# Narrow matmuls in twos on the two row halves, and the running sums of the decays moved into that stage

## The reference

```python
def _rwkv_bidir(u, v_first, vres, w0, w2, a0, a2, g2, k_k, k_a, r_k, gn_g, gn_b):
    r, k, v, wd_f, wd_b, ad_f, ad_b, gd = _split(u, [RW, RW, RW, 64, 64, 64, 64, 128])
    if vres is None: v_first = v
    else:
        v0, v1, v2 = vres
        v = v + (v_first - v) * jax.nn.sigmoid(v0 + (v @ v1) @ v2)   # v1: 512 x 32, v2: 32 x 512
    g = jax.nn.sigmoid(gd) @ g2
    kk = heads(k * k_k)
    kk = kk * lax.rsqrt(jnp.sum(kk * kk, -1, keepdims=True) + 1e-12)
    def direction(d, wd, ad, reverse):
        wl = w0[d] + jnp.tanh(wd) @ w2[d]                            # w2[d]: 64 x 512
        decay = jnp.exp(-jnp.exp(-jax.nn.softplus(-wl) - 0.5))
        a = jax.nn.sigmoid(a0[d] + ad @ a2[d])                       # a2[d]: 64 x 512
        kd = heads(k * (1.0 + (a - 1.0) * k_a))
        y = _wkv_scan(rh, heads(decay), kd, vh, kk, heads(a), reverse)
```

## Time and profile before

| | us |
|---|---|
| median of 3 runs (lowest, highest) | 4052.82 (4042.91, 4060.68) |
| the profiled execution | 4066.26 |
| its span in the profile | 4064.1 |
| TensorE busy | 3447.5 (85%) |
| VectorE busy | 1516.6 (37%) |
| ScalarE busy | 775.2 (19%) |
| mean granted TensorE clock | 0.91 |

### The profile page before, as it was taken

One profiled execution on the slowest core, in us unless ns is written; L12 is line 12 of the kernel. 1 busy time (PEld: TensorE's weight loads), 2 busy tenths in 40 slices (PEclk: granted clock), 3 DMA queues, 4 the chain that ended last, 5 costly groups with the idle time before them and its releaser, 6 DMA issues. The chain is left out here.

```text
span 4064.1 us, 74254 instructions
## 1 busy us (share of the span) xinstructions
PE 3447.5 (85%) x32128; PEld 2321.4 (57%) x32128; DVE 1516.6 (37%) x2765; ACT 775.2 (19%) x1578; POOL 329.0 (8%) x499
## 2 busy tenths in 40 slices
PE   4899899958856998898868847679989899999998
PEld 0666798754435666898645424447657744444443
DVE  2343555441122444454421132355456621144411
ACT  3112222121101113222111111013342210010000
POOL 0000221001110001220011110000023100000000
PEclk7999799968977997999969978889999999999999
DMA  8200300139972001101079932010010032222221
GB/s 297 77 32 23 126 5 5 43 119 376 397 279 86 32 16 76 76 4 41 5 290 373 409 110 73 16 44 21 21 54 1 1 122 74 73 72 73 70 59 47
DMA packets 178106, 418.33 MB, mean 103 GB/s; under 512 B 32661, under 2 KB 125205, under 8 KB 149253
## 3 DMA queue, kind: packets, MB, share of 16 engines
q1 hardware_dynamic: 158821, 379.68, 25.3%
q0 software_dynamic: 8736, 17.32, 1.6%
q10 hardware_dynamic: 10240, 16.79, 1.3%
HBM read 397.01 MB, written 50.54 MB: 110 GB/s over the span
## 5 line engine op out<-in xcount | busy, mean ns | idle before, releaser
L3213 PE MATMUL ps<-h_lat,wt 128*128 128x512 f32 x704 | 304.4, 595 | 5.9 <-ACT h_lat L3270 5.9
L1971 PE MATMUL ps<-e_w,e_xt 128*64 128x256 f32 x1792 | 236.3, 423 | 75.7 <-DMA e_w<-in_moe_w 75.6
L1971 PEld LDWEIGHTS ps<-e_w,e_xt 128*64 128x64 f32 x1792 | 156.4, 153 | 179.0 <-issue 98.8
L708 PE MATMUL ps<-h,win 128*128 128x264 f32 x960 | 232.7, 396 | 17.3 <-DVE pad L857 15.7
L3213 PEld LDWEIGHTS ps<-h_lat,wt 128*128 128x128 f32 x704 | 134.5, 191 | 175.8 <-issue 174.4
L708 PEld LDWEIGHTS ps<-h,win 128*128 128x128 f32 x960 | 180.5, 193 | 67.7 <-issue 39.1
L2078 DVE TENSOR_TENSOR e_hid<-ps,e_silu 64x256 f32<-64x256 f32 x64 | 39.3, 614 | 416.3 <-ACT e_silu L2037 416.3
L3170 PE MATMUL ps<-h_lat,wt 128*128 128x512 f32 x384 | 169.0, 598 | 10.9 <-DMA wt<-in_w_in 10.9
L3231 PE MATMUL ps<-ff_up,wt 128*128 128x512 f32 x352 | 152.2, 592 | 0.0
L1284 PE MATMUL ps<-inv,nt 48*48 48x48 f32 x3520 | 129.9, 207 | 12.6 <-issue 11.0
L1388 DVE COPY_PREDICATED inv<-level,ps 112x384 f32<-112x384 int32 x176 | 103.5, 588 | 85.8 <-PE ps L1284 77.6
(11 more groups left out here) (566 smaller groups left out, 6441.9 us busy)
## 6 DMA issues: line engine op xcount, KB each, us to landing
e_w<-in_moe_w SPq DMA_DIRECT2D x168, 1024.0 KB, 13.5
wmod<-in_w_mod SPq DMA_DIRECT2D x24, 1024.0 KB, 14.2
early<-in_moe_w SPq DMA_DIRECT2D x24, 1024.0 KB, 16.5
wt<-in_w_up SPq DMA_DIRECT2D x22, 1024.0 KB, 5.1
y_rows<-e_y ACTq DMA_DIRECT2D x128, 128.0 KB
win<-in_w_in SPq DMA_DIRECT2D x10, 1536.0 KB, 6.6
wt<-in_w_in SPq DMA_DIRECT2D x12, 1024.0 KB, 7.7
wt<-in_w_down SPq DMA_DIRECT2D x16, 704.0 KB, 4.8
```

The lines of the kernel that those rows point to most:

```text
L708: last = pe.matmul(ps[:, 7, 0:HT], lhsT=ring[(s + 1) % 2][:, i, o:o + P], rhs=k.h[:, i, h * HT:(h + 1) * HT], start=(i == 0), stop=(i == K ...
L1971: last = pe.matmul(ps[half, 2 + z, 0:EH], lhsT=xt[z][:, f, :], rhs=w[:, f, :], start=(f == 0), stop=(f == KD - 1))
L3213: last = pe.matmul(o, lhsT=w[:, i, m % 2 * P:(m % 2 + 1) * P], rhs=hl[:, i, :], start=(i == 0), stop=(i == KD - 1))
```

## The change

In `rwkv_prep`:

- The slots come in another order: `low` first, alone, then fourteen pairs: `sig` (4), `mix` (2), `rate` (4), `kk` (2), `att` (2). The two slots of a pair have their operands on different row halves. For `sig` and `rate` these are the two directions of one tile of channels. For `mix`, `kk` and `att` the operands are made twice, on rows from 0 and from 64: `v2` is loaded twice, `v1` is loaded twice into a tile of 96 columns (the 32 in the middle blank), `sel` has its 12 columns twice among 128, so `v_low` and `prep_root` come out on both halves.
- The matmuls of a pair alternate: first half of the positions of both slots, then the second half. Before a pair starts, both of its slots must be free.
- The sums stand between `sig` and `mix`. The squares of the attention output follow the `sig` evictions. The square root stands on ScalarE after the `mix` evictions, the tanh of `decay_in` first of all.
- The eight scans are done here, each after its `sig` eviction; VectorE's subtraction for `v` stands after the fourth. The reciprocal stands after the update of the first tile of `v`.

In `wkv` the scans and ScalarE's two waits on them are gone.

```diff
-        slots = ([("rate", d, m) for d in range(2) for m in range(RT)] + [("low", 0, 0)]
-                 + [("mix", 0, m) for m in range(RT)] + [("sig", d, m) for d in range(2) for m in range(RT)]
-                 + [("kk", 0, i) for i in range(RT)] + [("att", 0, h) for h in range(H_A)])
+        slots = ([("low", 0, 0)] + [("sig", d, m) for m in range(RT) for d in range(2)]
+                 + [("mix", m % 2, m) for m in range(RT)] + [("rate", d, m) for m in range(RT) for d in range(2)]
+                 + [("kk", i % 2, i) for i in range(RT)] + [("att", h % 2, h) for h in range(H_A)])
...
-                sp.dma_start(v1[:, :, :], a["rwkv_v1"][0].rearrange("(t p) n -> p t n", p=P)).then_inc(small_in, 16)
-                sp.dma_start(v2[:, :], a["rwkv_v2"][0]).then_inc(small_in, 16)
+                for b in (0, E):
+                    sp.dma_start(v2[b:b + LOW, :], a["rwkv_v2"][0]).then_inc(low_in, 16)
+                sp.wait_ge(low_blank, 1)
+                for b in (0, E):
+                    sp.dma_start(v1[:, :, b:b + LOW], a["rwkv_v1"][0].rearrange("(t p) n -> p t n", p=P)
+                                 ).then_inc(low_in, 16)
...
+                def pair(t):
+                    for x in (t, t + 1):
+                        if x >= 3:
+                            pe.wait_ge(act_emptied if by_act[x - 3] else dve_emptied, upto(x - 3))
+                    for h in range(2):
+                        hs = slice(h * HT, (h + 1) * HT)
+                        for x in (t, t + 1):
+                            l, r = operands(*slots[x])
+                            last = pe.matmul(two(x)[:, h, :], lhsT=l, rhs=r[:, hs], start=True, stop=True)
+                            if h:
+                                last.then_inc(slot_made, 1)
+                pe.wait_ge(low_in, 16 * 4)
...
+                for t in range(1, len(slots), 2):
+                    if t == MIX:
+                        sums()
+                        pe.wait_ge(act_emptied, 1)
...
+                    pair(t)
...
+                def scan(t):
+                    kind, d, m = slots[t]
+                    dve.wait_ge(act_emptied, t + 1)
+                    o, keep = sig[d][:, m, :], k.reset[:, d:d + T]
+                    if d:
+                        o, keep = o[:, ::-1], keep[:, ::-1]
+                    dve.tensor_tensor_scan(o, keep, o, 0.0, ALU.mult, ALU.add).then_inc(scanned, 1)
...
-                        if c < 2:
-                            act.wait_ge(scanned, RT * (d + 1))
...
-                    for f in range(RT):
-                        o, m = sig[d][:, f, :], k.reset[:, d:d + T]
-                        if d:
-                            o, m = o[:, ::-1], m[:, ::-1]
-                        dve.tensor_tensor_scan(o, m, o, 0.0, ALU.mult, ALU.add).then_inc(scanned, 1)
```

More of the change, by code:

```diff
@@ L947, in two @@
             return ps[:, 2 * (t % 3):2 * (t % 3) + 2, 0:HT]
[L948 to L951, removed]
+        with k.stage("low_in", "v_out", "v_in", "tanh_made", "gate_made", "att_squared", "keyed", "summed", "rooted",
+                     "inverted", "slot_made", "act_emptied", "dve_emptied", "y_blank", "low_blank", "sel_set", "eps_set",
+                     "spread_set", "scanned", "pool_chain", "prep_chain") as (
+                block, low_in, v_out, v_in, tanh_made, gate_made, att_squared, keyed, summed, rooted, inverted,
+                slot_made, act_emptied, dve_emptied, y_blank, low_blank, sel_set, eps_set, spread_set, scanned,
+                pool_steps, steps):
             @block.sync
@@ new lines, in sums @@
+                def sums():
+                    pe.wait_ge(att_squared, H_A)
+                    pe.wait_ge(keyed, RT)
+                    pe.wait_ge(sel_set, H_A + RT)
+                    for h in range(2):
+                        for n in range(H_A + RT):
+                            last = pe.matmul(ps[:, 6 + h, 0:HT], lhsT=sel[:, n, :, :].rearrange("p b e -> p (b e)"),
+                                             rhs=sq[:, n, h * HT:(h + 1) * HT], start=(n == 0), stop=(n == H_A + RT - 1))
+                    last.then_inc(summed, 1)
@@ new lines, in operands @@
+                def operands(kind, d, m):
+                    c, b = slice(m * P, (m + 1) * P), slice(64 * d, 64 * d + 64)
+                    if kind == "rate":
+                        return k.a2[b, c], rate_in[b, :]
+                    if kind == "sig":
+                        return k.w2[b, c], decay_in[b, :]
+                    if kind == "mix":
+                        b = slice(E * d, E * d + LOW)
+                        return v2[b, c], low[b, :]
+                    b = slice(E * d, E * d + H_A + H_B)
+                    if kind == "kk":
+                        return spread[b, 2 * m:2 * m + 2, :].rearrange("p b n -> p (b n)"), root[b, :]
+                    return few[b, m:m + 1].to_broadcast([H_A + H_B, P]), root[b, :]
@@ new lines, in _ @@
+                pe.wait_ge(low_in, 16 * 4)
+                for h in range(2):
+                    for i in range(RT):
+                        last = pe.matmul(two(0)[0:E + LOW, h, :], lhsT=v1[:, i, :], rhs=v[:, i, h * HT:(h + 1) * HT],
+                                         start=(i == 0), stop=(i == RT - 1))
+                last.then_inc(slot_made, 1)
+                pe.wait_ge(tanh_made, 1)
+                for t in range(1, len(slots), 2):
+                    if t == MIX:
+                        sums()
+                        pe.wait_ge(act_emptied, 1)
+                    if slots[t][0:2] == ("kk", 0) and slots[t][2] == 0:
+                        pe.wait_ge(inverted, 1)
+                        pe.wait_ge(spread_set, 1)
+                    pair(t)
```

120 lines of the change are left out of this document (44 added, 76 removed).

## The result

| | before | after |
|---|---|---|
| median (range) of 20 runs each, us | 4052.07 (4041.16 to 4063.03) | 4067.72 (4052.05 to 4076.09) |
| ratio after / before, 95% interval | | 1.0034 [1.0024, 1.0045] |
| profiled execution, us (span) | 4066.26 (4064.1) | 4076.09 (4074.0) |
| stage in front of the scan, layer 0 / 1, us | 56.2 / 56.0 | 63.0 / 62.7 |
| from its end to the first matmul on `bet`, us | 15.8 / 15.8 | 13.2 / 13.2 |

The medians lie 15.6 us apart; the ratio says 0.34%, 14 us. That is inside the 0.5% that the prediction took for no change, but the interval of the ratio excludes 1: the kernel is a little slower, and the forecast was +1 us. In the table a stage goes from the start of its first operation to the end of its last eviction.

The account below looks back on a forecast made before the run. TensorE was taken to set the prep stage's length. Per layer, the stage 3.4 us longer less 3.0 us gained in `wkv` gave net +0.4, +0.8 for two: forecast 4054 us (chance 0.62), range 4037 to 4068.

Parts of the forecast that it names:

- the case that had 0.86: Whole kernel: time the same as before, meaning within 0.5%, 20 us; chance 0.86.
- first matmul, after the stage's start: Start of the prep stage: TensorE idles 5.6 us for four loads issued behind the 1056 KB store, bounds 5.1 and 7.0.
- `sig`, with the wait for the last square: Prep stage after `low`: table load, three cycles of 1.95 us, last eviction and square, 9.8 us together.
- end of the sums to the second `rate` pair: Prep stage: `mix`, then two table loads and the root no longer hidden; 8.55 us, TensorE idle some 3.5.
- from there to the last eviction: End of the prep stage: six half-clock cycles of 2.92 us, a last pair and two evictions, 21.2 us.
- gain at the start of `wkv`: Start of `wkv`: without the scans the first matmul on `bet` comes 3.0 us earlier per layer, bounds 2.4 and 3.1.
- After the 2 us gap I add 1.0 for a start at half clock: Sums in the prep stage: 1.0 us added to 7.28 for starting at half clock after idling, bounds 0 and 3.
- the first (clock at half in `sig`): Rival: clock stays at half in the `sig` pairs, +5 us per layer, 4064 us; chance 0.20.
- The second (tail at full clock): Rival: pairs from the second `rate` pair on run at full clock, saving 6.8 us per layer, 4040 us; chance 0.12.
- Rival 4: Prep stage: paired matmuls do not overlap after all, adding 46 us, 4100 us; chance 0.02.
- every term but `low` at its good end: Whole kernel: the sum of terms at their favourable bounds, given as 4035 us.
- GpSimd's new operations: Prep stage: an added memset and copy end some 12 us in, before the sums, with almost no wait on them.

Follow-up runs that it names:

- e3: Kernel after, but each slot waits only for its own bank and makes both its matmuls before the next slot; ratio 0.9975 to the kernel before.
- e5: Kernel after, with ScalarE's four squares of the attention output ahead of all evictions; ratio 1.0004 to the kernel before.
- e4: Kernel after, with the four small loads of `v1` and `v2` issued ahead of the 1056 KB store; ratio 1.0003 to the kernel before.
- e10: Kernel before, with only the order of the `rate` and `sig` slots changed so the two directions take turns; ratio 0.9929 to the kernel before.
- e7: Kernel after, with 64 rows instead of 12 per half in `kk` and `att`, zeros in the added rows; ratio 1.0018 to the kernel before.
- e8: Kernel after, with single slots, `sig` ahead of `low`, 64 rows in `kk` and `att`, square root ahead of `mix`; ratio 0.9878 to the kernel before.
- e11: The same kernel as e8, unchanged, timed again on another chip; ratio 0.9897 to the kernel before.

## Why the prediction was right or wrong

The time, 4067.7, lies in the range and in the case that had 0.86. That it stayed in the range is luck: by 0.3 us, with 5 to 7 us from outside the stretch that the prediction had worked out. The forecast itself is 14 us off. By its steps, layer 0:

| step | predicted | measured |
|---|---|---|
| first matmul, after the stage's start | 5.6 | 6.0 |
| `low` | 6.1 | 6.4 |
| `sig`, with the wait for the last square | 9.8 | 9.9 |
| sums | 8.3 (7.3 + 1.0) | 10.4 |
| end of the sums to the second `rate` pair | 8.55 | 8.7 |
| from there to the last eviction | 21.2 | 21.6 |
| stage | 59.6 | 63.0 |
| gain at the start of `wkv` | 3.0 | 2.6 |

- Right, and shown by rows: a pair takes 1.16 and 2.13 us, to the digit; a cycle 2.01 and 2.98 (said 1.95 and 2.92), as a pair has to wait for two slots; the table loads and the root that lay under the sums now stall TensorE for 3.46 us (said 3.5); nobody waits for the scans; the clock is 0.50 from the second `rate` pair on. Undoing the wait for two slots (e3) gave 11.3 us per layer, 10 of them outside the sums, so this is indeed what ate the overlap.
- The term that was mis-sized: "After the 2 us gap I add 1.0 for a start at half clock (bounds 0 and 3)". It was 3.1, and so 2.1 of the 3.4 us by which the stage's sum fell short (0.4 and 0.3 came from the first two lines and 0.4 from the tail). The mechanism was right: e5 takes the gap away, and the sums are back at 7.39 at full clock. The bounds were right too: behind the same gap the runs show 0.1 to 3.2, and 2.4 on average over ten layers. A start at half clock could have been read from the kernel before, where `low` took 6.26 us, and 4.84 in layer 1, for 16 records that take 3.6 at full clock: 1.2 to 2.6 us, and 1.0 was below both.
- Of the rivals, the first (clock at half in `sig`) didn't happen in either layer here. It did in layer 0 of e4, and its price was too high: a lengthened pair cost the 0.97 that it names or less, but there were two and not three, and the sums behind them took 9.11, less than the 10.43 here and not 2 more. The second (tail at full clock) is excluded at 0.50. But its reason against, that 12 rows hold the clock down with no gap at all, is too strong: in e10 `kk` ran its 12 rows at 1.00 for the first 4 us, and `att` at 0.50 after that. In this tail it was the gaps between pairs: 64 rows in pairs stayed at 0.50 (e7), 64 rows without gaps rose to 1.00 (e3). Without gaps the rows may count as well: with 64 of them `kk` and `att` stayed at 1.00 in e8 and e11 (405.00 to 415.30 above), with 12 `att` ran at 0.50 in both layers of e3; this was not tested apart. By the Trainium skill, "TensorE: Matmul & The Clock Gate", Why this matters for your kernels, idle gaps are what costs the clock; in the tail the runs agree in direction, with gaps of 0.85 us, while 64 rows without a gap at 0.50, in slots on one half, don't.
- Three figures of the prediction are off without changing its outcome. Rival 4 counts 1.76 us a pair, but a pair one matmul after another would take 3.52 against the 2.13 already in the sum, 1.39 more, which makes 4090 and not 4100. With every term but `low` at its good end the sum is 4037, not 4035. GpSimd's new operations ended 4.3 us into the stage, not 12.
- The stage and the start of `wkv` account for +8.3 us. The other 5 to 7 of the measured 14 to 16 were not predicted and are not explained.
- Nothing in the prediction asked what the overlap would be worth without the pairs. The earlier trace rows held the answer, two evictions in 1.50 us at the one place where single slots change halves, and the text read it as a proof for pairs.

## What to carry to other kernels

Two matmuls on different row halves overlap by being neighbours in TensorE's order; they don't have to be issued as a pair, and with a ring of three a pair gives up the lead that hides the evictions. Before building such a stage, reorder the list: two terms of it in another order were worth 29 us here, while the whole of pairing, doubled operands and moved scans cost 14. An idle time of 2 us on TensorE is to be priced with the half-clock stretch that may stand behind it: 0.1 to 3.2 us here, for one and the same gap. A small load that the first matmul needs goes ahead of a large store on its queue: 2.5 us here.

## What the runs showed of the hardware

- VectorE's scans and GpSimd's products at the start of `wkv` lengthen each other: the product for `bet` takes 1.46 us beside a scan and 0.59 without; four scans take 5.58 us there and 4.71 in the stage (timelines of e10, then of the kernel after; the 4.71 is in the first fence). The Trainium skill, "SBUF — State Buffer", SBUF: two separate sides, has a port pair that the two engines share, for which a VectorE operation with two inputs in SBUF, as the scan has, competes. The rows agree, though it was not tested apart.

```profile
421.43 5.58 DVE L1345 TENSOR_TENSOR_SCAN sig<-reset,sig 128x528 f32<-128x528 f32 x4
421.61 1.46 POOL L1176 TENSOR_TENSOR bet<-kk,rate 128x192 f32<-128x192 f32 x1 [37.53 <-DVE one_less L1338]
```
```profile
440.87 0.59 POOL L1205 TENSOR_TENSOR bet<-kk,rate 128x192 f32<-128x192 f32 x1 [58.90 <-DVE one_less L1365]
```

- Records of 12 rows ran at 1.00 for 4 us in e10, right behind a dense stretch, then at 0.50 without a gap between them (`att`, 6.78 us).
- One and the same kernel took 5 to 6 us more or less over 300 us of `wkv` in two executions (e8 and e11), and 34.6 or 36.7 us in the stage ahead of it in layer 0. Within one execution the two layers' stages differ by up to 3.2 us (e4). A single profile settles such a stage to 2 or 3 us, unless one compares it step by step.
